# A fused transformer kernel's first mixer: engine orders around the state scan rewritten, the scan's steps widened, the first weight chunk loaded in four pieces

## What is computed

```
hn = rms_norm(x, g);  z = hn @ ev_w_in                  # q, k, v, u, 512 wide each
att = dilated_attention(rope(q)/8, rope(k), v)          # 8 heads of 64, one masked softmax
a_bar = exp(A*dt);  b_bar = (a_bar-1)/A * B             # complex, 32 groups x 64 states
h[s] = a_bar * h[s-1] + b_bar @ u[s]                    # the state scan over 256 rows
y = gelu(real(C @ h) + d*u);  ssm = y * sigmoid(y @ w_glu)
mix = concat(att, ssm) @ ev_w_out;  x = x + rms_norm(mix, g2)
```

## Time and profile before

| | |
|---|---|
| median of 3 runs | 1376.28 us (1374.03 to 1376.49) |
| the profiled execution | 1378.56 us, span 1376.8 us |
| TensorE busy | 93%, mean granted clock 0.971 |
| VectorE, ScalarE, GpSimd busy | 60%, 49%, 4% |
| instructions | 15928 |

### The profile page before, as it was taken

The page is one execution under the profiler, slowest core; times in us unless marked ns, Lnnn a source line. Parts: engine busy times, 40 slices in busy tenths (PEclk is TensorE's granted clock), DMA queues, the critical chain, the costliest instruction groups (busy, mean ns, idle before and its releaser), DMA issues.

```text
span 1376.8 us, 15928 instructions
## 1 busy us (share of the span) xinstructions
PE 1285.7 (93%) x6374; PEld 1053.0 (76%) x6374; DVE 819.8 (60%) x1132; ACT 680.4 (49%) x1087; POOL 52.0 (4%) x67
## 2 busy tenths in 40 slices
PE   6888899999998989999999889999999969999998
PEld 5666688888786778888787668788887857788887
DVE  7793565563686675664567543766545664666643
ACT  6444354443568664443488733544435553544431
POOL 0110000000000010000012100000000100000000
...
GB/s 309 120 108 1 95 199 184 185 178 198 188 180 99 177 157 214 189 188 183 155 203 198 88 7 123 184 183 183 184 184 164 183 62 61 153 213 184 184 183 62
DMA packets 31962, 216.62 MB, mean 157 GB/s; under 512 B 3840, under 2 KB 4224, under 8 KB 6672
## 3 DMA queue, kind: packets, MB, share of 16 engines
...
## 4 chain that ended last, share of the span: by engine, by line
PE 76%; DVE 12%; ACT 8%; issue 3%; DMA 1%; POOL 1%; SPq 0%; DVEq 0%; ACTq 0%
PE PS L404 22%; PE PS L406 22%; PE PS L405 22%; PE PS L410 4%; DVE WL L1588 3%; ACT WH L1015 3%; PE PS L676 2%; PE PS L699 2%; ACT JK L1127 1%; ACT HTh L1028 1%; DVE HTl L1602 1%; DMA RAW<-in_w 1%; POOL st L2248 1%; PE PS L557 0%; DVE YG L1633 0%
## 5 line engine op out<-in xcount | busy, mean ns | idle before, releaser
L1588 DVE TENSOR_TENSOR WL<-RAW,WH 128x2048 fp32r<-128x2048 f32 (+1 forms) x200 | 451.1, 2260 | 397.9 <-ACT WH L1015 397.8
L1015 ACT ACTIVATE WH<-RAW 128x2048 fp32r<-128x2048 f32 (+1 forms) x200 | 377.3, 1891 | 443.9 <-PE PS L406 442.2
L404 PE MATMUL PS<-WH,HTh 128*128 128x512 f32 (+2 forms) x1008 | 399.7, 397 | 24.1 <-DVE WL L1588 13.4
L406 PE MATMUL PS<-WH,HTl 128*128 128x512 f32 (+2 forms) x1008 | 393.0, 390 | 0.0
L405 PE MATMUL PS<-WL,HTh 128*128 128x512 f32 (+2 forms) x1008 | 392.4, 389 | 0.0
L404 PEld LDWEIGHTS PS<-WH,HTh 128*128 128x128 f32 x1008 | 191.0, 190 | 64.7 <-DVE WL L1588 25.0
L406 PEld LDWEIGHTS PS<-WH,HTl 128*128 128x128 f32 x1008 | 190.6, 189 | 39.8
L405 PEld LDWEIGHTS PS<-WL,HTh 128*128 128x128 f32 x1008 | 191.2, 190 | 36.7
L404 PE MATMUL PS<-WH,YAh 128*128 128x512 f32 x386 | 153.2, 397 | 1.0 <-DVE WL L1588 0.6
L405 PE MATMUL PS<-WL,YAh 128*128 128x512 f32 x386 | 151.1, 391 | 0.0
L406 PE MATMUL PS<-WH,YAl 128*128 128x512 f32 x386 | 150.9, 391 | 0.0
...
## 6 DMA issues: line engine op xcount, KB each, us to landing
...
```

The source lines that it names most:

```text
L404: e.matmul(out, ah, bh, start=start, stop=False)
L406: return e.matmul(out, al, bh, start=False, stop=stop)
L1015: e.activation(WH[:, c % NW, w], RAW[:, c % NR, w], ACT.Copy).then_inc(S.hi, 1)
L1588: e.tensor_tensor(WL[:, c % NW, w], RAW[:, c % NR, w], WH[:, c % NW, w].bitcast(f32), SUB).then_inc(S.lo, 1)
```

## The change

Nothing that is computed changes, and nothing behind the first mixer. The parts:

- **Start.** SyncE issues the first half of X first, then the identity, then chunk 0 as four loads of 128x512 with semaphores of their own, then chunk 1, the second half of X, chunk 2. Three small loads (cst, pos, inv) go to ScalarE's queue. VectorE's split of chunk 1 stands ahead of its small coefficient operations, that of chunk 2 behind the second half's HTl; ScalarE's splits follow.
- **Wider operations.** `rotate(q)` is two products of 128x1024 and two subtractions of 128x512, with SX holding minus sine and sine (two sines on ScalarE in place of one); `scan(q)` is two scans of 128x512 over all four groups, with the decay read from a full tensor RT whose first column of each group is 0; the rotation back is two products of 128x1024.
- **GpSimd** fills RT (four copies of 128x512 and a memset, ahead of the first norm's power) and computes CFe (six operations of 128x512, ahead of the rotary turn).
- **Orders.** `rows_mm` on TensorE takes steps after any contraction step. The last scan tile ends ahead of the attention's first maximum; in the attention only `c_h(3)`, `skip(3)` and the split of chunk 10 are left; gelu and gating stand three heads earlier. TN, CP, CQ, SX and RT lie in memory that YAh and YAl take later.

Cut to its core (seg_a, seg_b and the hooks are deleted, late_c holds the six CFo operations as before):

```diff
+        with ExitStack() as sc:
+            scope.append(sc)
+            TN, CP_ = sb("TN", [128, 4, 128]), sb("CP", [128, 16, 32])
+            SX = sb("SX", [128, 2, 2, 4, 128])
+            CQ_, _ = sb("CQ", [128, 16, 32]), sb("YAlgap", [128, 512])
+            RT = sb("RT", [128, 16, 128])
+            scope.pop()
...
-            W = [sb(f"W{i}", [128, 4, 128]) for i in range(4)]
-            CT_, CU_ = (W[i][:, :, :].rearrange("p a (b c) -> p (a b) c", c=32) for i in range(2))
+            cosT = sb("cosT", [128, 2, 4, 128])
+            W = sb("W", [128, 4, 4, 128])
+            WAT = (0, 3, 2, 1)
...
+                    e.wait_ge(S.pp, PP["CF"])
                 else:
                     e.wait_ge(S.ssm, q)
-                e.wait_ge(S.w, 4 * q + 4)
+                e.wait_ge(S.w, 2 * q + 2)
...
             def attention0():
                 def step(h):
                     if h == 0:
-                        seg_b(2)
-                    elif h == 1:
-                        seg_a(3)
+                        c_h(3)
                     elif h == 3:
-                        c_h(3)
-                    elif h == 6:
                         glu()
...
-            rows_mm(PLAN["ev_q"], 4, 8, 512, HT, (2, 3), hook=behind_q)
-            rows_mm(PLAN["ev_k"], 4, 8, 512, HT, (0, 1), k_free, behind_k)
-            rows_mm(PLAN["ev_v"], 4, 8, 512, HT, (2, 3), v_free, behind_v)
+            rows_mm(PLAN["ev_q"], 4, 8, 512, HT, (2, 3), at={1: [u_turn], 2: [b_first]})
+            rows_mm(PLAN["ev_k"], 4, 8, 512, HT, (0, 1), k_free,
+                    at={0: [lambda: b_u(1)], 1: [direct_terms], 2: [lambda: c_h(0)], 4: [lambda: b_u(2)]})
+            rows_mm(PLAN["ev_v"], 4, 8, 512, HT, (2, 3), v_free,
+                    at={0: [lambda: c_h(1), lambda: b_u(3)], 3: [q_turn], 5: [lambda: c_h(2)], 6: [k_turn]})
...
+            e.dma_start(cst[:, :], A["cols"][:, :]).then_inc(S.c_c, 16)
+            e.dma_start(pos[:, :], A["pos"][:, :]).then_inc(S.c_p, 16)
+            e.dma_start(inv[:, :], A["tab"][:, 896:904]).then_inc(S.c_i, 16)
...
-            e.wait_ge(S.w0, 16)
             for i in range(4):
+                e.wait_ge((S.w0a, S.w0b, S.w0c, S.w0d)[i], 16)
...
-                e.activation(Sn, TN[:, :, :], ACT.Sin, scale=-6.283185)
+                for r in range(2):
+                    e.activation(Sn[:, r, :, :], TN[:, :, :], ACT.Sin, scale=(-6.283185, 6.283185)[r])
...
+            edge_mm(PLAN["ev_u"], 0, lambda: [angles(0), angles(1)])
+            e.wait_ge(S.rs, RSTD["row0"])
+            evac_in("ev_u", (0, 1), Qn)
+            feed(PLAN["ev_u"][1])
+            pairs(0, uT, (4, 5))
...
+            table(0)
+            feed(PLAN["ev_q"][0])
+            table(1)
+            e.wait_ge(S.uq, 2)
+            evac_in("ev_q", (2, 3), Qn)
+            feed(PLAN["ev_q"][1])
+            angles(2)
+            e.wait_ge(S.k0p, 1)
...
+            table(2)
+            feed(PLAN["ev_k"][0])
...
-                    if h == 0:
-                        seg_b(2)
-                    elif h == 1:
-                        seg_a(3)
+                    if h == 1:
+                        gelu()
                     elif h == 4:
-                        gelu()
-                    elif h == 7:
                         c = PLAN["glu"][0]
...
+            feed(-2)
...
+            def rotate(q):
+                b = PS[:, 4:6, :].rearrange("p b (h r t) -> p r (b h) t", h=2, r=2)
+                Gq, C = G[:, q % 2, :, :, :], cosT[:, q % 2, :, :].unsqueeze(1).to_broadcast([128, 2, 4, 128])
...
+                e.tensor_tensor(Gq, b, C, MUL).then_inc(S.dv, dv.up())
+                e.tensor_tensor(T2, b, SX[:, q % 2, :, :, :], MUL).then_inc(S.bread, 1)
...
+                for r in range(2):
+                    e.tensor_tensor(Gq[:, r, :, :], Gq[:, r, :, :], T2[:, 1 - r, :, :], SUB).then_inc(S.dv, dv.up())
...
-                for j in range(4):
-                    rj = R2[:, 4 * q + j:4 * q + j + 1].to_broadcast([128, 128])
-                    e.tensor_tensor_scan(A0[:, j, :], rj, A0[:, j, :], 0.0, MUL, ADD).then_inc(S.dv, dv.up())
-                    e.tensor_tensor_scan(A1[:, j, :], rj, A1[:, j, :], 0.0, MUL, ADD).then_inc(S.dv, dv.up())
...
+                for r in range(2):
+                    e.tensor_tensor_scan(flat(Gq[:, r, :, :]), flat(RT[:, 4 * q:4 * q + 4, :]), flat(Gq[:, r, :, :]), 0.0, MUL, ADD).then_inc(S.dv, dv.up())
...
-                e.tensor_tensor(W[0][:, :, :], A0, C, MUL).then_inc(S.w, 1)
-                e.scalar_tensor_tensor(W[1][:, :, :], A1, -1.0, Sn, MUL, MUL).then_inc(S.w, 1)
-                e.tensor_tensor(W[2][:, :, :], A0, Sn, MUL).then_inc(S.w, 1)
-                e.tensor_tensor(W[3][:, :, :], A1, C, MUL).then_inc(S.w, 1)
...
+                e.tensor_tensor(W[:, 0:2, :, :], Gq, cosT[:, q % 2, :, :].unsqueeze(1).to_broadcast([128, 2, 4, 128]), MUL).then_inc(S.w, 1)
+                e.tensor_tensor(W[:, 2:4, :, :], Gq, SX[:, q % 2, :, :, :], MUL).then_inc(S.w, 1)
...
+            turn(0, 1)
+            feed(PLAN["ev_u"][0] - 1)
+            row_var(0)
+            late_b()
+            feed(PLAN["ev_u"][0])
+            table(0)
+            feed(PLAN["ev_u"][1])
+            late_c()
+            rotate(0)
+            table(1)
+            scan(0)
+            feed(PLAN["ev_q"][0])
+            rotate(1)
+            table(2)
+            skip(0)
+            scan(1)
+            feed(PLAN["ev_q"][1])
+            rotate(2)
+            table(3)
+            skip(1)
+            scan(2)
+            feed(PLAN["ev_k"][0])
+            rotate(3)
+            skip(2)
+            scan(3)
+            feed(PLAN["ev_k"][1])
+            feed(PLAN["ev_v"][0])
...
-                    if h == 0:
-                        seg_b(2)
-                    elif h == 1:
-                        seg_a(3)
+                    if h == 1:
+                        skip(3)
+                        feed(PLAN["ev_v"][1])
                     elif h == 2:
-                        seg_b(3)
-                    elif h == 3:
-                        skip(3)
+                        gelu_lo()
                     elif h == 5:
...
+            e.wait_ge(S.pd, PD["R2"])
+            for q in range(4):
+                e.tensor_copy(RT[:, 4 * q:4 * q + 4, :].rearrange("p (b h) t -> p b h t", b=2),
+                              R2[:, 4 * q:4 * q + 4].rearrange("p (h b) -> p b h", h=2).unsqueeze(3).to_broadcast([128, 2, 2, 128])).then_inc(S.rt, 1)
+            e.wait_ge(S.rt, 4)
+            e.memset(RT[:, :, 0:1], 0.0).then_inc(S.rtz, 1)
             power("row0", 2, 2)
...
+            e.wait_ge(S.pd, PD["CF"])
+            wide16 = lambda a: a.unsqueeze(2).to_broadcast([128, 16, 32])
+            ar, ai = wide16(ARE), wide16(SN)
+            e.tensor_tensor(CFe[:, 0, :, :], CFo[:, 0, :, :], ar, MUL).then_inc(S.pp, 1)
+            e.tensor_tensor(CP_[:, :, :], CFo[:, 1, :, :], ai, MUL).then_inc(S.pp, 1)
...
+            e.tensor_tensor(CFe[:, 0, :, :], CFe[:, 0, :, :], CP_[:, :, :], ADD).then_inc(S.pp, 1)
+            e.tensor_tensor(CFe[:, 1, :, :], CFo[:, 1, :, :], ar, MUL).then_inc(S.pp, 1)
+            e.tensor_tensor(CQ_[:, :, :], CFo[:, 0, :, :], ai, MUL).then_inc(S.pp, 1)
...
+            e.tensor_tensor(CFe[:, 1, :, :], CFe[:, 1, :, :], CQ_[:, :, :], SUB).then_inc(S.pp, 1)
...
-            e.dma_start(cst[:, :], A["cols"][:, :]).then_inc(S.c_c, 16)
+            e.dma_start(X[:, 0, :], A["x"][0:128, :]).then_inc(S.c_x0, 16)
             e.dma_start(ident[:, :], A["tab"][:, 0:128]).then_inc(S.c_id, 16)
-            e.dma_start(X[:, 0, :], A["x"][0:128, :]).then_inc(S.c_x0, 16)
-            e.dma_start(pos[:, :], A["pos"][:, :]).then_inc(S.c_p, 16)
-            e.dma_start(inv[:, :], A["tab"][:, 896:904]).then_inc(S.c_i, 16)
-            weights(0)
+            e.dma_start(RAW[:, 0, 0:512], A["w"][0, :, 0:512]).then_inc(S.w0a, 16)
+            e.dma_start(RAW[:, 0, 512:1024], A["w"][0, :, 512:1024]).then_inc(S.w0b, 16)
...
+            weights(1)
             e.dma_start(X[:, 1, :], A["x"][128:256, :]).then_inc(S.c_x1, 16)
-            weights(1)
```

246 lines of the change are left out of this document (82 added, 164 removed).

## The result

The changed kernel takes **1366.16 us** (median of 4 runs, 1362.46 to 1367.8) beside 1375.63 for the kernel before on the same chip: a ratio of 0.9929, 95% interval 0.9906 to 0.9951, 9.5 us less. A second comparison gave 1367.45 beside 1374.68, 0.9942 (0.9926 to 0.9958). The forecast was 1355.0 with a range of 1346 to 1364: the direction was right, the gain was less than half of what was forecast, and the range missed it. TensorE is busy 1283.5 us (94%), against the earlier trace rows.

A forecast was written before the change was run, and what follows sets the result against it. Ahead of the output product no engine is full and they wait in turns, a microsecond off VectorE being worth about one. Output product from 146.1 to 124.8, 21.3 us less, gave a median of 1355.0 us, range 1346 to 1364.

The forecast's parts named there:

- Sharing: VectorE slowed while GpSimd works, through shared SBUF interfaces: about a fifth more, 2.5 us, bounds 0.5 and 4.
- The start: VectorE reaches the first coefficient product at 24.1, bounds 22 to 25; ScalarE's first exponential about a microsecond later.
- Attention: From first maximum at 90.4 to output product at 124.8, against 146.11 before; three heads more at 2.3 us each.
- the earlier gate: End of the attention: 1.0 us comes back since the gated half is copied before the last heads.
- order, not width: Scan and rotation on VectorE: widening alone worth 0.8 us a tile; it is the order that matters.
- rival 2: Rotation's 128x1024 products: wide PSUM reads lose their rate, adding 9.2 us; gain 12.1, time 1364; chance 10%.
- rival 3: GpSimd's CFe products become the bound; slower beyond 6.1 us each, 1388 at 8; 3%, plus 2% for no change.
- the skip term's wait of 1.7: Tile 3 on VectorE: the skip term waits 1.7 us for C product 2 on TensorE, until 78.4.
- nothing lost behind the output product: Behind the output product: unchanged and TensorE's own work, so the 21.3 us gain stays.
- Rival 1: The end of the attention keeps its length; only its start moves, by 7.9 us, giving 1368; chance 7%.
- Rival 4: No contention (2.5 us) and the first product's 2 us passed on: gain 25.8, time 1350; chance 13%.

The follow-up runs named there:

- cst first: Changed kernel with the load of the small constants (cst) put back first on SyncE's queue: 1365.25 us, ratio 0.9927.
- again: The changed kernel itself, unedited, profiled and timed a second time beside the kernel before: 1367.45 us, ratio 0.9942.
- CFe on VectorE: Changed kernel with the six products of CFe moved back from GpSimd to VectorE, behind CFo: 1366.7 us, ratio 0.9937.
- early products: Gate late kernel plus TensorE products nobody reads, 6 before head 0's turn and 12 before head 1's: 1361.87 us, ratio 0.9899.
- gate late: Changed kernel with gate and weight split 11 moved behind head 5's maximum and the first division on VectorE: 1362.99 us, ratio 0.9911.
- the clock held: Early products kernel plus three more unread products ahead of the turns of heads 4, 5 and 6: 1359.41 us, ratio 0.9872.

## Why the prediction was wrong

By its own steps, in us (measured: the first profile of the changed kernel; the last column: what an experiment gives with one cause taken away):

| step | forecast | measured | cause taken away |
|---|---|---|---|
| start to first coefficient product | 24.1 | 25.6 | 23.9, cst first |
| to first rotation | 13.4 | 13.4 | |
| to first maximum | 52.9 | 56.0 (again 55.1) | 51.8, CFe on VectorE |
| to gating product | 9.0 | 10.6 | 9.2, early products |
| gating product | 7.8 | 8.1 | |
| to output product | 17.6 | 21.3 | 19.7, gate late; 17.9, and the clock held |
| sum | 124.8 | 135.0 | |

- **Sharing was the first wrong term.** I took a fifth more time while both engines work, from 0.83 for 0.69 us, 2.5 us in all. There GpSimd's instructions were 128 elements long. Its new ones have 512, and a VectorE instruction that was caught beside them lost 0.7 to 0.9 us, nearly the 1.05 of one of them, whatever its own length. Four were caught beside CFe: 3.4 us by their own durations, 3.3 to 4.2 by the distance to the first maximum, for CFe alone. The rotary turn's short instructions cost little each (a product of 1.48 for 1.22 at 50.73), by VectorE's rows 1.6 us in all, 0.9 in the second profile. Without any sharing the forecast had 50.4 us from first rotation to first maximum; 56.0 and 55.1 were measured. The value taken was too small and the bound of 4 too near; GpSimd's own products (1.05 to 1.50) were rightly bounded and their end at 46.75 hidden, as forecast.
- **The start** was outside its bounds of 22 to 25, in both profiles of the changed kernel. I counted the later exponential as a microsecond and then let it vanish among the splits. It did not, and I gave no time to the other loads on ScalarE's queue: with cst at its head, VectorE reached the first coefficient product 1.7 us later than without, 0.5 us for the exponential and the larger part in a wait for `inv`, the last of the three.
- **Attention, the largest term.** I priced a head at 2.3 us, from one gap of the earlier trace rows, and used it in a stretch whose clock stood at 0.67 in the earlier trace rows. At 1.2 GHz a turn, a value and a score product fill 3.58 us and TensorE itself is the bound between them. With the gate late and the clock held, this part takes 17.9 us, so at 2.4 GHz the forecast's 17.6 was nearly right. Second, I credited the earlier gate with 1.0 us; the new places cost 1.8, of which 1.6 is the gate and split in front of head 5's maximum. I never walked VectorE's queue there, as I had done for the scan.
- **Right:** order, not width, carries the gain; 128x1024 reads of PSUM at 1.22 and 1.21 (rival 2 falls); CFe at most 1.50, done at 46.75 (rival 3 falls); the skip term's wait of 1.7; nothing lost behind the output product.
- **Rival 1** gave 1368, close to the measured time, but not by its mechanism: the end of the attention went from 47.8 to 40.0 us, and its start moved by 3.3, not 7.9. Rival 4 fell on both counts.

The errors all went one way: 1.5 + 3.1 + 1.6 + 0.3 + 3.7 = 10.2 us. The forecast's own range was nearly the plain sum of its bounds, so it was not the adding up that failed. Each bound was too near: 0.9 us upward for the start, 1.5 for the sharing, 3 for the attention, against 1.5, 3.1 and 5.6. The median missed by 11.2 us; the last microsecond is spread between a profiled execution and a median.
